# A two-block transformer in fp32 on one Trainium2 core: other distances between the slots of two SBUF rings

## The reference

```python
def reference(x, c, positions, ...):
    x = first_block(...)      # 2 layers: modulated rmsnorm, hybrid mixer, swiglu
    return second_block(x, ...)  # 2 layers: MoBA or dilated attention, squared-relu MLP

# first block, per layer l
mod = (silu(c) @ ada_w[l] + ada_b[l])            # 6 * 1024 modulation values
h = rmsnorm(x, norm1_g[l]) * (1 + sc1) + sh1
x = x + g1 * hybrid_mixer(h, ...)                # proj = h @ w_in + b_in, 16 heads of 3 kinds, w_branch, w_out
h = rmsnorm(x, norm2_g[l]) * (1 + sc2) + sh2
x = x + g2 * ((silu(h @ Wg) * (h @ Wu)) @ w_ffn_out[l])
# second block, per layer i
h = layer_norm(a * h + attention_i(h @ w_qkv) @ w_o, ...)
h = layer_norm(a * h + square(relu(h @ w_in)) @ w_out, ...)
```

## Time and profile before

| | |
|---|---|
| median of three runs | 1510.87 us |
| span of the profiled execution, first to last instruction | 1507.4 us |
| PE busy | 1466.3 us, 97% |
| PEld busy | 1237.5 us |
| POOL busy | 1203.5 us, 80% |
| DVE busy | 769.8 us |
| ACT busy | 717.4 us |
| DMA | 313.88 MB, mean 208 GB/s |
| mean granted clock of TensorE | 0.996 |

### The profile page before, as it was taken

The page is one execution under the profiler, slowest core; times in us unless marked ns, Lnnn a source line. Parts: engine busy times, 40 slices in busy tenths (PEclk is TensorE's granted clock), DMA queues, the critical chain, the costliest instruction groups (busy, mean ns, idle before and its releaser), DMA issues.

```text
span 1507.4 us, 21800 instructions
## 1 busy us (share of the span) xinstructions
PE 1466.3 (97%) x7762; PEld 1237.5 (82%) x7762; DVE 769.8 (51%) x1594; ACT 717.4 (48%) x1154; POOL 1203.5 (80%) x968
## 2 busy tenths in 40 slices
PE   7999999999999999999999999999999999999997
PEld 3898887799978987888788887878888887788886
DVE  7576755666643758655566304264550044555202
ACT  3345554544444344554544444364554345455432
POOL 4799988788888977548798997917999978279994
PEclk9999999999999999999999999999999999999999
DMA  9995546689866985425676565624565656146653
GB/s 357 317 396 176 188 142 192 221 297 337 313 218 203 375 287 173 134 85 186 212 258 203 188 204 164 211 81 128 194 196 196 210 168 211 54 157 207 193 192 105
DMA packets 149685, 313.88 MB, mean 208 GB/s; under 512 B 10933, under 2 KB 31817, under 8 KB 149577
## 3 DMA queue, kind: packets, MB, share of 16 engines
q1 hardware_dynamic: 147824, 311.15, 62.5%
q10 hardware_dynamic: 1754, 1.35, 0.3%
HBM read 311.39 MB, written 1.06 MB: 207 GB/s over the span
## 4 chain that ended last, share of the span: by engine, by line
PE 89%; DVE 5%; ACT 2%; POOL 2%; DMA 1%; issue 1%; SPq 0%; DVEq 0%; ACTq 0%
PE bank L717 54%; PE bank L760 11%; PE bank L761 8%; PE bank L758 5%; POOL lo_units L674 2%; PE bank L905 2%; PE bank L926 1%; PE bank L894 1%; PE bank L893 1%; PE bank L892 1%; PE bank L944 1%; DMA raw_units<-in_w_out 1%; ACT hi_units L1181 1%; DVE bank L1509 1%; PE bank L796 1%
## 5 line engine op out<-in xcount | busy, mean ns | idle before, releaser
L674 POOL TENSOR_TENSOR lo_units<-raw_units,hi_units 128x512 fp32r<-128x512 f32 (+3 forms) x928 | 1153.8, 1277 | 269.5 <-ACT hi_units L1181 267.9
L1181 ACT ACTIVATE hi_units<-raw_units 128x1024 fp32r<-128x1024 f32 (+1 forms) x470 | 483.3, 1031 | 438.5 <-PE bank L717 227.0
L717 PE MATMUL bank<-hi_units,turned 128*128 128x512 f32 (+3 forms) x1600 | 508.1, 389 | 4.6 <-POOL lo_units L674 3.0
L717 PEld LDWEIGHTS bank<-hi_units,turned 128*128 128x128 f32 x1600 | 301.5, 189 | 61.8 <-POOL lo_units L674 4.1
L717 PE MATMUL bank<-hi_units,turned_wide 128*128 128x512 f32 x992 | 309.8, 391 | 1.9 <-DVE turned_wide L1557 1.9
L717 PE MATMUL bank<-lo_units,turned 128*128 128x512 f32 (+3 forms) x800 | 307.0, 384 | 0.0
L761 PE MATMUL bank<-turned,lo_units 128*128 128x256 f32 x1024 | 288.1, 281 | 0.0
L760 PE MATMUL bank<-turned,hi_units 128*128 128x512 f32 x736 | 260.1, 398 | 0.0
L717 PEld LDWEIGHTS bank<-hi_units,turned_wide 128*128 128x128 f32 x992 | 186.3, 188 | 41.4 <-DVE turned_wide L1557 2.2
L761 PEld LDWEIGHTS bank<-turned,lo_units 128*128 128x128 f32 x1024 | 194.3, 190 | 0.2
L717 PE MATMUL bank<-lo_units,turned_wide 128*128 128x512 f32 x496 | 193.1, 389 | 0.0
(11 more groups left out here) (249 smaller groups left out, 1383.3 us busy)
## 6 DMA issues: line engine op xcount, KB each, us to landing
ada_units<-in_ada_w SPq DMA_DIRECT2D x88, 512.0 KB, 7.6
raw_units<-in_w_ffn_tiles SPq DMA_DIRECT2D x72, 512.0 KB, 5.1
raw_units<-in_mlp_w_out SPq DMA_DIRECT2D x64, 512.0 KB, 3.3
raw_units<-in_mlp_w_tiles SPq DMA_DIRECT2D x56, 512.0 KB, 3.3
raw_units<-in_w_in SPq DMA_DIRECT2D x56, 458.0 KB, 7.4
raw_units<-in_w_in SPq DMA_DIRECT2D x48, 512.0 KB, 3.9
raw_units<-in_w_ffn_out SPq DMA_DIRECT2D x44, 512.0 KB, 3.3
raw_units<-in_moba_w_qkv SPq DMA_DIRECT2D x24, 512.0 KB, 3.7
```

The lines of the kernel that those rows point to most:

```text
L674: pool.tensor_tensor(LO[:, s, b, 0:w], RAW[:, u["slot"], b, 0:w], HI_[:, s, b, 0:w].bitcast(F32), ALU.subtract).then_inc(lo_ready.sem, lo_ ...
L717: ins = pe.matmul(BANK[2 * c["pair"] + t][:, 0:w], xs[:, part, :], W[:, s, b, 0:w], start=(i == 0 and m == 0 and q == 0), stop=(i == len(c ...
L1181: act.activation(HI_[:, s, 0:n, 0:w], RAW[:, u["slot"], 0:n, 0:w], ACT.Copy)\
```

## The change

The rows of `hi_units` and `lo_units` get a gap behind each slot, 16 elements (64 bytes) for high and 4 elements (16 bytes) for low. The views HI_ and LO that all engines use leave the gap out, so that no instruction, count, wait or order changes. The dynamic DMA scratch goes from its default of 16384 bytes in each partition to 1024, and everything in SBUF moves with `nc.sbuf_base`.

```diff
+HI_GAP, LO_GAP = 16, 4
...
-    HI_, _ = place("hi_units", [P, NH, UNIT_K, CW], F32R)
-    LO, _ = place("lo_units", [P, NH, UNIT_K, CW], F32R)
+    HI_ROWS, _ = place("hi_units", [P, NH, UNIT_K * CW + HI_GAP], F32R)
+    LO_ROWS, _ = place("lo_units", [P, NH, UNIT_K * CW + LO_GAP], F32R)
+    HI_, LO = (a[:, :, 0:UNIT_K * CW].rearrange("p s (k n) -> p s k n", k=UNIT_K) for a in (HI_ROWS, LO_ROWS))
...
-    traced(bacc.Bacc("TRN2", target_bir_lowering=False, num_devices=1), arrays, cat, ({}, values))
-    nc = traced(bacc.Bacc("TRN2", target_bir_lowering=False, num_devices=1), arrays, cat, (values, {}))
+    traced(bacc.Bacc("TRN2", target_bir_lowering=False, num_devices=1, dynamic_dma_scratch_size=1024), arrays, cat, ({}, values))
+    nc = traced(bacc.Bacc("TRN2", target_bir_lowering=False, num_devices=1, dynamic_dma_scratch_size=1024), arrays, cat, (values, {}))
```

## The result

The changed kernel takes 1519.71 us, the median of 4 runs (1517.72 to 1520.62), against 1509.97 for the kernel before, the median of 4 on the same chip. The ratio is 1.0062, with a 95% interval of 1.0049 to 1.0075: slower by 9.7 us.

The account below looks back on a forecast made before the run. PE's matmul spacing was taken as the bound; terms of +8.5, +3.4, -1.0, -1.5 and 0 gave +9.4 us on the 1507.4 us span, 1516.8, plus 3.5 for the median of the runs: 1520 us, range 1493 to 1531.

Parts of the forecast that it names:

- What bounds the kernel: PE, with 89% of the chain of waits; only the distance between two matmul starts counts, changed through PE's read addresses.
- Scratch, gaps on ACT and POOL: nothing: Smaller scratch costs nothing; padding effects on ACT and POOL stay hidden behind waits and don't reach PE: 0 us.
- Term 1: 512-column matmuls on L717 take 231.8 ns, as just after a change of product: +8.5 us in long pieces, +3.4 elsewhere.
- Term 2: 864 matmuls of 256 columns, L758 and L761 of the first block, go from 120.0 to 118.9 ns: -1.0 us.
- Term 3: 736 pairs on L760 and L761, second MLP's tiles, go from mostly 353.3 toward 350.7 ns: -1.5 us, at most -1.9.
- Term 4: Matmuls of 458 and 456 columns are in no even step before the change, so nothing changes: 0 us.
- The sum: All terms together add 9.4 us, and all of it reaches the end because PE waits for nobody in long pieces.
- Rival A: Gaps take PE's two read streams apart, so 512-column matmuls get faster: -15 us, 1496 us; chance 0.33.
- Rival B: PE's rhythm finds itself again at any offset, or gains and losses between slots cancel: 1511 us; chance 0.14.
- Rival C: Low halves at 16-byte steps and turned_wide at 32 make L717's 512-column matmuls 234.2 ns: 1530 us; chance 0.13.
- Differences by slot: A sign to look for: matmul distances on PE differing by ring slot and repeating every five units; no size given.
- The reading behind it: PE's moving operand and next weights are read together and meet in SBUF; cost depends on offsets, 13.4 ns over 512 columns.

Follow-up runs that it names:

- the two kernels made for it: Scratch cut to 1024 bytes against the kernel before, once without gaps (1510.91 us, ratio 1.0002), once with both gaps 256 bytes (1510.53 us, ratio 1.0004).

## Why the prediction was right

- **What bounds the kernel.** Held. The loss is in the distances on PE, with POOL's and ACT's work unchanged, and a PE with no other engine at work shows it as well.
- **Scratch, gaps on ACT and POOL: nothing.** Held, 1.0002 and 1.0004 by the two kernels made for it.
- **Term 1, an uneven offset costs what a restart costs.** Held in size: +12.3 us where +11.9 was summed. 231.8 ns was taken from the restart; the two long pieces took 232.1 and 232.2. The split held less well: the long pieces lost 9.5 us and not 8.5, the rest 2.8 and not 3.4, 2.1 ns a matmul where 2.6 was taken. That the restart gave the price is in part luck. A restart is a way in that ends, after which the series at the common offset are at 226.7 ns; an uneven offset is a lasting state, mostly of 228.9 to 236.7 ns by the offset and the entry, whose mix over the slots here comes to 232. No run shows why the two should be alike.
- **Term 2, 256 columns.** Held: -1.2 us where -1.0 was taken.
- **Term 3, the pairs.** Right in sign, small in size: -2.1 us where -1.5 was taken and -1.9 called the most. The limit was wrong: 350.7 ns was added up from two kinds of matmul, but most of the five slots lie below it, down to 346.9. That pairs can also change their rhythm at unchanged offsets wasn't in the prediction at all.
- **Term 4, 458 columns: nothing.** A small miss, +0.8 us. They were not so free of a rhythm as I read: 208.3 ns in most pieces before, which PE alone gives at the common offset too (208.5), and mostly 209.4 to 210.1 after. The prediction had itself found 833.3 ns for four of them among its whole multiples, which doesn't go with calling them free.
- **The sum.** +9.4 was predicted, +9.7 measured between the medians, +8.5 on the profiled span.
- **Rival A, streams kept apart.** Fell. In some 60 series of PE alone no offset settled under 226.7 ns for 512 columns. At 0.33 I gave it more than the trace bore. The 13.4 ns over the columns was read as the cost of a meeting that an offset could spare; it is there at the best offset and grows at the others. The Trainium skill's formula, 215.8 ns at 512 columns and there called the gap of an isolated matmul (TensorE: Matmul & The Clock Gate, section "Back-to-back issue gap"), was reached nowhere here, with PE alone as little as in the kernel.
- **Rival B, nothing moves.** Fell. After the change PE doesn't find 226.7 again in pieces of 378 matmuls.
- **Rival C, worse at 16-byte steps.** Not seen as a mean. Single series do reach 234.7 to 236.7 ns, but the long pieces stay at 232, and the low gap alone, in 16-byte steps, gave 231.5.
- **Differences by slot**, which I had said would show offsets at work, are there and small: 230.5 to 233.2 ns among the high halves against turned, and the pairs repeat every five units.
- **The reading behind it**, that the moving operand and the next weights meet in SBUF, isn't shown. It led to the right place, for the distance of their two offsets decides, but the price follows the weights' columns at 240 bytes alone and stays with one tile read again and again. What the 5 ns are within PE is open.

## What to carry to other kernels

Where a kernel is bound by full-rate matmuls, look at the byte offset in 256 of both operands: with 128 columns of weights, all at one common multiple of 32 gave 226.7 ns for 512 columns, anything else mostly 229 to 234, or 1 to 3% of the time. A gap between buffers that isn't a multiple of 256 bytes gives that away without one added instruction. The even step of a long piece, with a single duration for all its matmuls, is the sign that the rhythm holds, and the places in the same trace where it doesn't hold (a restart, a buffer at another offset) gave its price before any run.

## What the runs showed that I had not expected

The kernel after has a DVE instruction of 21.7 us in which no operand is a ring: one of six products of x_rows and mod_rows into a bank. This is the line in the kernel before, then in the kernel after (duration min/median/max in ns), and what POOL did around 451.1 us, when the long one starts.

```profile
L1588 DVE TENSOR_TENSOR bank<-x_rows,mod_rows x6: 687/782/3427, 274.6 to 718.3; 128x512 f32<-128x512 f32 x6
```

```profile
L1590 DVE TENSOR_TENSOR bank<-x_rows,mod_rows x6: 687/696/21674, 275.8 to 720.0; 128x512 f32<-128x512 f32 x6
```

```profile
444.91 27.32 POOL L676 TENSOR_TENSOR lo_units<-raw_units,hi_units 128x512 fp32r<-128x512 f32 x22
```

POOL's 22 subtractions follow each other without a pause until 472.2 us, and the DVE instruction ends at 472.8. It reads SBUF twice. The Trainium skill has this in SBUF — State Buffer, section "Who interferes with whom": a DVE instruction with both inputs in SBUF contends with a GpSimd instruction that reads there. The trace agrees in kind. What decides whether it is held up wasn't found: in the kernel before, the same two instructions took 0.9 and 1.8 us beside the same row of subtractions. The kernel with the smaller scratch alone has the long one (21.9 us), the one with 256-byte gaps has not. It has no visible part in the loss: in the kernel after, PE then waits 0.26 us for DVE, and in the kernel with the smaller scratch alone 1.1 us, whose time is that of the kernel before. The long instruction makes up nearly all of the 22 us more that DVE is busy.
